# First block of a hybrid network in another order, and the first mixer tiles on what is unmasked

## The chip, the cores and the metric

One core of one Trainium2 chip computes all of it. The time is the device time in microseconds of that core for one execution. The kernel before was timed in three runs.

## The reference

`x` is 512 tokens by 1024 channels, in fp32. One first block is followed by two layers of a second kind. Cut to what matters here:

```python
def first_block(x, ...):
    z = rms_norm(x, norm1_g) @ w_in                    # 1024 -> 2304 columns
    y_a = gmlp_mixer(z[..., :512])                     # u * (masked ws @ layer_norm(gelu(v)))
    y_b = rglru_mixer(z[..., 512:768], z[..., 768:1024])  # convolution, gates, linear scan
    y_c = hgrn2_mixer(q, f, i, g)                      # att_ts = sum_d q_td k_sd exp(b_td - b_sd)
    y_d = pool_mixer(z[..., 2048:])                    # means over 2, 4, 8, 16 tokens
    x = x + concatenate([y_a, y_b, y_c, y_d]) @ w_out
    ...                                                # feed-forward, gated embedding

def hybrid_layer(x, ...):
    proj = rms(x) * norm1_g @ w_in
    o_a = sliding_window_attention(aq, ak, av, sinks) @ w_attn_o   # window 128, blocks of 128
    o_b = rwkv7_time_mix(rw, ...) @ w_rwkv_o
    o_c = retention(rq, rk, rv, rg) @ w_ret_o                      # chunks of 128, a running state
    x = x + (g0 * o_a + g1 * o_b + g2 * o_c) @ w_out
    ...                                                            # gated feed-forward
```

In the attention the first block of 128 queries sees no earlier block: its 128 keys before position 0 are masked. In the retention the state before the first chunk is zero, and the state after the last is not used.

## The kernel before, in words

Tensors lie with channels on 128 partitions and tokens in 512 columns. Every large weight comes as 128-column tiles of fp32. SP loads a tile pair into `raw` (two buffers, s = 0 and 1), POOL makes of it a rounded part `w_hi` (line 347) and a rest `w_lo` (line 354), and PE computes a *slot* (`slot`, three passes of eight matmuls, or of four where the input has four channel groups): `w_hi` by the input's high part, `w_hi` by its low part, `w_lo` by its high part, all summed in the accumulator `acc[s]`. Nearly all matmuls go through one helper, line 475. A slot may begin when POOL has split its weights (`w_split`) and DVE has emptied its accumulator (`acc_free`). A pair is the slots of s = 0 and 1.

The order of the work on each engine is written out by hand, and the engines meet at semaphores. In the first block, `w_in` has nine pairs, numbered 0 to 8. Their order is that of a list at the end of the file: input of the convolution, gate of the scan, `v` of the gated mixer, `u`, forget gate, query, value, output gate, input of the pooling. DVE empties the two accumulators of a pair one after the other in `take`. PE does pairs 1 and 2, the gates of the scan (`wa`, `wx`), pair 3, transposes of `v` (line 594), pairs 4 and 5, the mixing over time (`ws`), pairs 6 and 7, and then the seven levels of the forget-gated attention and an eighth round for the diagonal.

That attention is computed by levels: at level `lev`, tokens in the second half of a group of 2 x 2^lev see those in the first half. DVE makes differences of the running sum of log gates (`decays`), ACT turns them into factors (absolute value, exponential), DVE multiplies queries and keys with them (`decayed`), PE forms scores of all groups (round `lev`, semaphore `sc`), and DVE copies the chosen ones to `att` (`chosen`, copies with a predicate, line 1331; ACT copies those of levels 5 and 6). The differences of level lev + 1 are made in round lev. In between lie pair 8, four pairs of half of `w_out` on what is ready of the mixers' outputs (`yy`; DVE adds them to `x` in `partial`), and the states between chunks (`states`, `added`). Then come the end of that attention, the head sums (`headones`), and `late` and `slots` for the other half of `w_out`.

DVE's other steps there: the convolution (line 1200, three times two operations), 26 operations on two columns for the scan's constant (line 1206 to 1233, `lam` and `lp`), normalisation of `v` (to `vn`), and the scan itself (line 1279).

In a layer of the second kind, a retention over four chunks (`rt_`) and an attention over four tiles (`an_`) follow the third mixer, with projection slots for gates and outputs laid between their parts. `rt_R` is the running state, `rt_qx` the decayed queries, `rt_kz` the decayed keys, `an_s` the scores, `an_pT` the transposed probabilities.

```python
def slot(s, I, a, chunks, early=False):
    ...
    pe.wait_ge(w_split[s], I + 2)
    pe.wait_ge(acc_free[s], I + 1)
```

## Time and profile before

| | before |
| --- | --- |
| median of three runs | 2688.89 us (2687.46 to 2690.88) |
| profiled execution | 2691.99 us |
| span of the profile | 2690.2 us |
| mean granted clock of TensorE | 0.992 |
| DMA | 222.67 MB, 83 GB/s on average |

The profiled execution took 1.8 us more than its span and 3.1 us more than the median. In rows of a timeline stand the start and the duration in us, the engine, the line, the operation with output and inputs, how many instructions are merged in the row, and in brackets how long the engine stood idle before it and what ended that. One fp32 matmul appears as two records. The granted clock is a share of the full 2.4 GHz.

### The profile page before, as it was taken

To read this page: it belongs to the slowest core of one execution; us is meant where nothing else is said; L and a number is where in the kernel's file an instruction comes from. 1 tells how busy PE (TensorE), PEld (TensorE's weight loads), DVE (VectorE), ACT (ScalarE), POOL (GpSimd) and SP (SyncE) were. 2 spreads that over 40 slices of the span, in tenths; PEclk is the share of its full clock that TensorE was granted. 3 is DMA by queue.
4 is the path that set the end of the run, shared out by engine and by line. 5 is a ranking of instruction groups with operands and counts; after the bars stand their busy time and mean duration, and the time that the engine had idled before them with its cause. 6 is when DMAs were issued, how large, how long until landed. Compare 5 with 4: busy or idle time off the path is not lost.

```text
span 2690.2 us, 47577 instructions
## 1 busy us (share of the span) xinstructions
PE 2607.9 (97%) x16458; PEld 2037.5 (76%) x16458; DVE 1474.7 (55%) x2059; ACT 634.4 (24%) x1159; POOL 1488.9 (55%) x945
## 2 busy tenths in 40 slices
PE   7888999999999999999999999999999999999999
PEld 5776888877676677787888887776677777888887
DVE  6776737364566637774442424557647774443434
ACT  2333000013224423541200002234423431200002
POOL 4564565655544444546666665654444546666665
PEclk9999999999999999999999999999999999999999
DMA  4212333323321122223333333311122223333332
GB/s 151 67 44 86 94 94 94 94 86 92 93 64 49 40 90 63 66 73 93 94 94 94 94 94 108 94 57 48 49 84 67 71 73 96 94 94 94 94 94 94
DMA packets 72726, 222.67 MB, mean 83 GB/s; under 512 B 9345, under 2 KB 12545, under 8 KB 72577
## 3 DMA queue, kind: packets, MB, share of 16 engines
q1 hardware_dynamic: 72576, 220.63, 27.2%
q8 instruction: 100, 1.64, 0.3%
q14 instruction: 50, 0.40, 0.0%
HBM read 218.50 MB, written 2.10 MB: 82 GB/s over the span
## 4 chain that ended last, share of the span: by engine, by line
PE 89%; DVE 4%; DVEq 2%; issue 2%; DMA 1%; POOL 1%; POOLq 1%; ACT 1%; ACTq 0%; SPq 0%
PE acc L475 78%; PE bank L475 10%; DMA raw<-in_w_pg 1%; PE bank L1046 0%; POOL w_lo L354 0%; DVEq L1526 0%; DVE rw_bon L1084 0%; DVE rw_SCB L1084 0%; DVE z_rw L1084 0%; DVEq L1619 0%; DMA x<-in_x 0%; DVE rw_AR L1617 0%; POOL w_hi L347 0%; PE bank L1006 0%; DVE z_rw L1564 0%
## 5 line engine op out<-in xcount | busy, mean ns | idle before, releaser
L354 POOL TENSOR_TENSOR w_lo<-raw,w_hi 128x1024 fp32r<-128x1024 f32 (+3 forms) x438 | 966.0, 2206 | 302.7 <-PE acc L475 282.3
L347 POOL TENSOR_SCALAR w_hi<-raw 128x1024 fp32r<-128x1024 f32 (+3 forms) x438 | 431.9, 986 | 714.8 <-PE acc L475 604.7
L475 PE MATMUL acc<-xg_hi,w_hi 128*128 128x512 f32 x2224 | 597.2, 406 | 37.6 <-issue 16.7
L475 PE MATMUL acc<-xg_hi,w_lo 128*128 128x512 f32 x2224 | 587.9, 399 | 0.0
L475 PE MATMUL acc<-xg_lo,w_hi 128*128 128x512 f32 x2224 | 586.2, 399 | 0.0
L475 PEld LDWEIGHTS acc<-xg_hi,w_hi 128*128 128x128 f32 x2224 | 414.4, 190 | 156.2 <-issue 62.3
L475 PEld LDWEIGHTS acc<-xg_lo,w_hi 128*128 128x128 f32 x2224 | 417.6, 189 | 104.2 <-issue 5.1
L475 PEld LDWEIGHTS acc<-xg_hi,w_lo 128*128 128x128 f32 x2224 | 414.9, 188 | 99.9
L1899 ACT ACTIVATE ffn_act<-ffn_t 128x512 f32<-128x512 f32 x100 | 63.3, 633 | 778.2 <-DVEq L1144 619.6
L1084 DVE TENSOR_TENSOR x<-x,acc 128x512 f32<-128x512 f32 x104 | 71.4, 688 | 316.3 <-PE acc L475 315.6
L475 PE MATMUL acc<-hid_hi,w_hi 128*128 128x512 f32 x656 | 182.7, 396 | 3.7 <-POOL w_lo L354 1.6
L475 PE MATMUL acc<-hid_hi,w_lo 128*128 128x512 f32 x656 | 182.1, 395 | 0.0
L475 PE MATMUL acc<-hid_lo,w_hi 128*128 128x512 f32 x656 | 181.9, 395 | 0.0
L475 PEld LDWEIGHTS acc<-hid_hi,w_hi 128*128 128x128 f32 x656 | 123.1, 188 | 37.4 <-issue 6.8
L1084 DVE TENSOR_TENSOR ffn_sq<-acc,rstd 128x512 f32<-128x512 f32 x44 | 30.4, 692 | 212.3 <-PE acc L475 212.3
L475 PEld LDWEIGHTS acc<-hid_hi,w_lo 128*128 128x128 f32 x656 | 123.2, 188 | 29.9
L475 PEld LDWEIGHTS acc<-hid_lo,w_hi 128*128 128x128 f32 x656 | 123.2, 188 | 29.5
L1084 DVE TENSOR_TENSOR ffn_t<-acc,rstd 128x512 f32<-128x512 f32 x100 | 69.2, 692 | 125.1 <-PE acc L475 108.0
L1916 ACT ACT_TABLE_LOAD x96 | 123.2, 1283 | 5.0 <-issue 2.1
L1084 DVE TENSOR_TENSOR ffn_h<-ffn_act,ffn_sq 128x512 f32<-128x512 f32 x44 | 96.1, 2183 | 11.6 <-issue 11.6
L1899 ACT ACTIVATE ffn_act<-bank 128x512 f32<-128x512 f32 x22 | 13.2, 599 | 314.8 <-DVEq L1438 314.8
L457 POOL TENSOR_TENSOR x<-x,z_rt 128x1024 f32<-128x1024 f32 x8 | 19.0, 2377 | 119.9 <-DVEq L1526 119.9
(342 smaller groups left out, 2839.6 us busy)
## 6 DMA issues: line engine op xcount, KB each, us to landing
raw<-in_w_up SPq DMA_DIRECT2D x132, 512.0 KB, 3.6
raw<-in_w_down SPq DMA_DIRECT2D x48, 512.0 KB, 3.6
raw<-in_w_gate SPq DMA_DIRECT2D x48, 512.0 KB, 3.6
raw<-in_w_ret SPq DMA_DIRECT2D x32, 512.0 KB, 3.6
raw<-in_w_rw SPq DMA_DIRECT2D x28, 512.0 KB, 3.6
raw<-in_w_o SPq DMA_DIRECT2D x48, 256.0 KB, 2.6
raw<-in_w_in SPq DMA_DIRECT2D x18, 512.0 KB, 3.6
raw<-in_w_down SPq DMA_DIRECT2D x24, 384.0 KB, 3.0
```

Of the source, the lines that this page charges most:

```text
L347: nc.gpsimd.tensor_scalar(w_hi[:, s, 0:n], raw[:, s, 0:n], 1.0, 0.0, ALU.mult, ALU.add).then_inc(w_half[s], 1)
L354: nc.gpsimd.tensor_tensor(w_lo[:, s, 0:n], raw[:, s, 0:n], bits(w_hi[:, s, 0:n]), ALU.subtract).then_inc(w_split[s], 1)
L457: nc.gpsimd.tensor_tensor(x[:, 2 * j:2 * j + 2, :], x[:, 2 * j:2 * j + 2, :], z_rt[:, 15:16, :].to_broadcast([P, 2, T]), ALU.mult)
L475: return nc.tensor.matmul(o, a, b, start=first, stop=last, skip_group_check=shared)
L1084: return v.tensor_tensor(o, a, b, op)
L1899: return nc.scalar.activation(o, i, f, **kw)
L1916: nc.scalar.preload_act_table_set(name)
```

## The change

In the first block the forget gate's pair moves from fifth to third (number 2), the pairs of `v` and `u` follow it, and the log gates, their running sum and the differences of level 0 are made ahead of the normalisation of `v`. `take` empties one accumulator instead of two, and the two halves of a pair are taken at different places. Differences are made two levels ahead. Pairs 7 and 8 are done by PE one slot at a time in the first four level rounds, three pairs of `w_out` in rounds 4 to 6, and the fourth in two halves at the end. The transposes of the decayed keys and the states move to levels 4 and 5. The absolute value for the log gates is computed by ACT, where DVE computed it before, and ACT loads one more table; `gelu` and `silu` steps of ACT stand in another order. POOL splits the four pairs of `w_out` one place later each.

In the mixers of each layer: tile 0 of the attention leaves out its masked half (scores, maximum, exponentials, transposes, value products), chunk 0 of the retention leaves out the product with the zero state, and chunk 3 the update of the state. Two memsets go.

```diff
@@ -605,9 +609,10 @@
                     last = mm(bank[2 + 2 * k + j][:], K[name][:, j, :], m1["ta"][:, j, :], True, True)
             last.then_inc(s1["ri"], 1)
             pair(3)
-            pe.wait_ge(s1["z"], 3)
+            slot(0, 4, xg, full)
+            pe.wait_ge(s1["z"], 4)
             transposed(0, m1["tg"])
-            pair(4)
+            slot(1, 4, xg, full)
             pair(5)
...
             last.then_inc(s1["sv"], 1)
             pair(6)
-            pair(7)
...
-                    pair(8)
+                if lev < 4:
+                    slot(lev % 2, 7 + lev // 2, xg, full)
...
-                if 2 <= lev < 6:
-                    if lev == 2:
-                        pe.wait_ge(y_ready, 4)
-                    for s in range(2):
-                        slot(s, B1_IN + lev - 2, yy, four)
...
+                if 4 <= lev < 7:
+                    if lev == 4:
+                        pe.wait_ge(y_ready, 4)
+                    for s in range(2):
+                        slot(s, B1_IN + lev - 4, yy, four)
...
             last.then_inc(s1["dwy"], 1)
+            slot(0, B1_IN + 3, yy, four)
             for j in range(2):
                 pe.wait_ge(s1["osq"], j + 1)
                 head_sums(bank[j][:], m1["ta"][:, j, :]).then_inc(s1["on"], 1)
+            slot(1, B1_IN + 3, yy, four)
             rest = range(4, DC)
...
+                            seen = P if n == 0 else 0
+                            last = mm(bank[2 * p + j // 2][:, (j % 2) * 2 * P + seen:(j % 2 + 1) * 2 * P], z_at[r, j, n * P:(n + 1) * P],
+                                      an["k"][r, j // 2, n * P + seen:(n + 2) * P], True, True)
...
+                    if n < NT - 1:
+                        for j in range(4):
+                            last = nc.tensor.transpose(bank[4][:, j * P:(j + 1) * P], rt["kr"][:, j, :], K["ident"][:])
...
+                    if n > 0:
+                        for j in range(4):
+                            js = slice(j * P, (j + 1) * P)
+                            mm(bank[0][:, js], rt["R"][:, j, :], rt["qx"][:, j, :], j == 0, False, True)
...
+                    if n < NT - 1:
+                        for j in range(4):
+                            js = slice(j * P, (j + 1) * P)
+                            last = mm(bank[1][:, js], rt["kz"][:, js], rt["vt"][:, js], True, True)
...
-                            for b in range(2):
+                            for b in blocks(n):
                                 last = nc.tensor.transpose(bank[2 * p + j // 2][:, (2 * (j % 2) + b) * P:(2 * (j % 2) + b + 1) * P],
...
-                        for b in range(2):
+                        for b in blocks(n):
                             last = mm(bank[4][p * HD:(p + 1) * HD, j * P:(j + 1) * P], an["v"][:, b, kv * HD:(kv + 1) * HD],
-                                      an["pT"][:, 4 * p + j, b, :], b == 0, b == 1)
+                                      an["pT"][:, 4 * p + j, b, :], b == blocks(n)[0], b == 1)
...
-            def take(i, dst):
-
-                for s in range(2):
-                    scaled(s, i, dst[:, s, :]).then_inc(acc_free[s], 1)
-                dve.drain()
-                dve.sem_inc(s1["z"], 1)
-
-            take(0, z[:, 2:4, :])
+            def take(i, s, dst):
+
+                scaled(s, i, dst[:, s, :]).then_inc(acc_free[s], 1)
+                if s == 1:
+                    dve.drain()
+                    dve.sem_inc(s1["z"], 1)
...
@@ -1200,6 +1212,8 @@
                     v.scalar_tensor_tensor(m1["ta"][:, j, :], m1["td"][:, j, 13 + k:13 + k + T], col(U_CW + 4 * j + k),
                                            m1["ta"][:, j, :], ALU.mult, ALU.add)
                 dve.drain()
+                if k == 0:
+                    take(1, 0, z[:, 4:6, :])
             dve.sem_inc(s1["conv"], 1)
...
+            take(1, 1, z[:, 4:6, :])
...
-            take(2, m1["tg"])
+            zf = z[:, 8:10, :]
+            for s in range(2):
+                take(2, s, zf)
 
...
+            tt(m1["ta"][:], m1["ta"][:], z[:, 16:18, :])
             dve.drain()
             dve.sem_inc(s1["mlt"], 1)
-            take(3, z[:, 0:2, :])
...
+            take(3, 0, m1["tg"])
 
             dve.wait_ge(s1["sil"], 1)
-            v.scalar_tensor_tensor(m1["ta"][:], zf, 0.0, m1["tf"][:], ALU.min, ALU.subtract)
-            dve.drain()
+            v.scalar_tensor_tensor(m1["th"][:], zf, 0.0, m1["tf"][:], ALU.min, ALU.subtract)
+            take(3, 1, m1["tg"])
             lf = m1["td"][:, :, 0:T]
             for j in range(2):
-                v.tensor_tensor_scan(lf[:, j, :], K["reset128"][:], m1["ta"][:, j, :], 0.0, ALU.mult, ALU.add)
-
...
+                v.tensor_tensor_scan(lf[:, j, :], K["reset128"][:], m1["th"][:, j, :], 0.0, ALU.mult, ALU.add)
             dve.drain()
             dve.sem_inc(s1["free"], 1)
...
             decays(0)
-            take(6, m1["th"])
+            take(4, 0, z[:, 0:2, :])
+            dve.wait_ge(s1["scan"], 1)
+            tt(m1["tb"][:], m1["tb"][:], z[:, 16:18, :])
+            dve.drain()
+            dve.sem_inc(s1["hx"], 1)
...
+            take(4, 1, z[:, 0:2, :])
...
+            take(5, 0, z[:, 6:8, :])
+
...
             decays(1)
+            take(5, 1, z[:, 6:8, :])
+            tt(m1["tb"][:], m1["tb"][:], z[:, 4:6, :])
+            dve.drain()
+            for j in range(2):
+                splitted(y_hi[:, 2 + j, :], y_lo[:, 2 + j, :], m1["tb"][:, j, :])
...
+            tt(z[:, 0:2, :], m1["tg"][:], z[:, 0:2, :])
+            dve.drain()
+            take(6, 0, m1["th"])
+
+            dve.wait_ge(s1["qs"], 1)
             for lev in range(7):
-                dve.wait_ge(s1["hl"], lev + 2)
+                dve.wait_ge(s1["hl"], lev + 1)
                 if lev == 1:
                     dve.wait_ge(s1["vT"], 2)
                 decayed(lev)
-                dve.sem_inc(s1["qk"], 1)
-                if lev == 0:
-
-                    for j in range(2):
-                        splitted(y_hi[:, j, :], y_lo[:, j, :], m1["tg"][:, j, :])
-                    dve.drain()
-                    dve.sem_inc(y_ready, 4)
...
+                dve.sem_inc(s1["qk"], 2 if lev == 6 else 1)
                 if 0 < lev < 6:
                     chosen(lev - 1)
-                    decays(lev + 1)
-                if 2 < lev < 6:
-                    partial(lev - 3)
-                if lev == KV_LEV + 1:
-                    added(range(1))
-                if lev == KV_LEV + 2:
-                    added(range(1, NT - 1))
-            dve.sem_inc(s1["qk"], 1)
-            partial(3)
+                if lev == 0:
+                    take(6, 1, m1["th"])
+                if lev < 5:
+                    decays(lev + 2)
+                if lev in (1, 2):
+                    j = lev - 1
+                    splitted(y_hi[:, j, :], y_lo[:, j, :], z[:, j, :])
+                    dve.drain()
+                    dve.sem_inc(y_ready, 2)
+                    take(7, j, z[:, 10:12, :])
+                if lev in (3, 4):
+                    take(8, lev - 3, z[:, 12:14, :])
+                if lev == 5:
+                    partial(0)
+            added(range(NT - 1))
+            partial(1)
+            partial(2)
...
-                    tt(rt["qx"][:], rt["qr"][:], K["xi"][:])
+                    if n > 0:
+                        tt(rt["qx"][:], rt["qr"][:], K["xi"][:])
...
-                    mask = K["atmask"][:, n, :]
+                    seen = slice(0 if n else P, 2 * P)
+                    mask = K["atmask"][:, n, seen]
...
-    d["w1_in"] = slots(f["w_in"], [4, 5, 6, 7, 2, 3, 0, 1, 10, 11, 8, 9, 12, 13, 14, 15, 16, 17])
+    d["w1_in"] = slots(f["w_in"], [4, 5, 6, 7, 10, 11, 2, 3, 0, 1, 8, 9, 12, 13, 14, 15, 16, 17])
```

PE, ahead of the first round of scores. `ws,z` is the mixing over time, `m_tb,m_tc` the scores of level 0, `acc` rows are passes of slots. The kernel before, from the first pass of pair 7:

```order
L475 MATMUL acc<-xg_hi,w_hi 128x512 x8
L475 MATMUL acc<-xg_lo,w_hi 128x512 x8
L475 MATMUL acc<-xg_hi,w_lo 128x512 x8
L475 MATMUL acc<-xg_hi,w_hi 128x512 x8
L475 MATMUL acc<-xg_lo,w_hi 128x512 x8
L475 MATMUL acc<-xg_hi,w_lo 128x512 x8
L475 MATMUL bank<-m_tb,m_tc 128x128 x16
L594 MATMUL bank<-ident,m_th 128x128 x8
L475 MATMUL acc<-xg_hi,w_hi 128x512 x8
L475 MATMUL acc<-xg_lo,w_hi 128x512 x8
```

The changed kernel, from the last pass of pair 6:

```order
L479 MATMUL acc<-xg_hi,w_lo 128x512 x8
L479 MATMUL bank<-m_tb,m_tc 128x128 x16
L598 MATMUL bank<-ident,m_th 128x128 x8
L479 MATMUL acc<-xg_hi,w_hi 128x512 x8
L479 MATMUL acc<-xg_lo,w_hi 128x512 x8
L479 MATMUL acc<-xg_hi,w_lo 128x512 x8
L479 MATMUL bank<-m_tg,m_th 128x128 x16
L479 MATMUL acc<-xg_hi,w_hi 128x512 x8
L479 MATMUL acc<-xg_lo,w_hi 128x512 x8
```

Pair 7 no longer stands ahead of the scores, and one slot of it follows each of the first two rounds.

DVE, between the factors of the gates and the normalisation of `v` (`z,lng`). `acc,rstd` is one accumulator taken, `reset_65` the running sum of log gates. Before:

```order
L1238 TENSOR_SCALAR z<-z,sml 128x512 x2
L1084 TENSOR_TENSOR m_ta<-m_ta,m_te 128x1024
L1084 TENSOR_TENSOR z<-acc,rstd 128x512 x2
L1248 BN_STATS sml<-z 128x6 x4
L1251 BN_AGGR sml<-sml 128x2 x4
L1084 TENSOR_TENSOR z<-acc,rstd 128x512 x2
L1084 TENSOR_TENSOR m_tb<-m_tb,m_td 128x1024
L1261 TENSOR_SCALAR z<-z,sml 128x256 x4
L1084 TENSOR_TENSOR z<-z,lng 128x1024
L1084 TENSOR_TENSOR z<-z,lnb 128x1024
L1271 SCALAR_TENSOR_TENSOR m_tf<-z 128x1024
```

Now:

```order
L1095 TENSOR_TENSOR m_ta<-m_ta,z 128x1024
L1095 TENSOR_TENSOR m_tg<-acc,rstd 128x512
L1261 SCALAR_TENSOR_TENSOR m_th<-z,m_tf 128x1024
L1095 TENSOR_TENSOR m_tg<-acc,rstd 128x512
L1265 SCALAR_TENSOR_TENSOR m_td<-reset_65,m_th 128x512 x2
L1095 TENSOR_TENSOR m_tf<-m_td 128x512 x2
L1095 TENSOR_TENSOR z<-acc,rstd 128x512
L1095 TENSOR_TENSOR m_tb<-m_tb,z 128x1024
L1333 BN_STATS sml<-z 128x6 x4
L1336 BN_AGGR sml<-sml 128x2 x4
L1095 TENSOR_TENSOR z<-acc,rstd 128x512
L1342 TENSOR_SCALAR z<-z,sml 128x256 x4
```

The running sum and the first differences (`m_tf<-m_td`) now stand ahead of the normalisation; before they came twelve and fifteen rows behind `z,lng`.

## Rows read from the trace of the kernel before

**Rows 1.** The profile's page, part 1: busy time of the engines.
```profile
PE 2607.9 (97%) x16458; PEld 2037.5 (76%) x16458; DVE 1474.7 (55%) x2059; ACT 634.4 (24%) x1159; POOL 1488.9 (55%) x945
```

**Rows 2.** Windows: length, busy of PE, PEld, DVE, ACT, POOL; PEclk, DMA share, GB/s.
```profile
24.33:214.55 190.22, 162.49 (x895) 128.18 (x895) 141.35 (x187) 59.05 (x74) 102.79 (x69) 0.94 0.21 64
1000.00:1200.00 200.00, 199.05 (x1118) 155.88 (x1117) 152.49 (x213) 89.77 (x170) 93.22 (x67) 1.00 0.23 67
```

**Rows 3.** Timeline of PE, first block: start us, us, operation, idle before.
```profile
46.47 3.43 PE L475 MATMUL acc<-xg_hi,w_hi 128*128 128x512 f32 x8 [4.11 <-issue]
...
62.31 2.42 PE L475 MATMUL acc<-xg_hi,w_hi 128*128 128x512 f32 x8
...
107.74 3.75 PE L475 MATMUL acc<-xg_hi,w_hi 128*128 128x512 f32 x8 [8.52 <-issue]
...
115.20 2.03 PE L475 MATMUL acc<-xg_hi,w_hi 128*128 128x512 f32 x8
...
120.80 2.03 PE L475 MATMUL acc<-xg_hi,w_hi 128*128 128x512 f32 x8
...
152.86 3.56 PE L475 MATMUL bank<-m_tb,m_tc 64*128 64x128 f32 x32 [3.21 <-DVEq L1332]
...
162.67 2.06 PE L475 MATMUL bank<-m_tg,m_th 64*128 64x128 f32 x32
...
214.55 0.77 PE L475 MATMUL acc<-y_hi,w_hi 128*128 128x512 f32 x1 [2.96 <-DVE y_lo L1084]
```

**Rows 4.** Timeline of DVE, first block.
```profile
54.33 2.21 DVE L1233 TENSOR_SCALAR sml<-sml 128x2 f32<-128x2 f32 x1
...
86.99 2.87 DVE L1084 TENSOR_TENSOR m_tb<-m_tb,m_td 128x1024 f32<-128x1024 f32 x1
...
95.54 1.23 DVE L1084 TENSOR_TENSOR z<-z,lnb 128x1024 f32<-128x1024 f32 x1
96.89 1.86 DVE L1271 SCALAR_TENSOR_TENSOR m_tf<-z 128x1024 f32<-128x1024 f32 x1
...
109.48 1.22 DVE L1288 SCALAR_TENSOR_TENSOR m_ta<-z,m_tf 128x1024 f32<-128x1024 f32 x1
110.78 2.34 DVE L1292 TENSOR_TENSOR_SCAN m_td<-reset,m_ta 128x512 f32<-128x512 f32 x2
...
116.10 3.24 DVE L1084 TENSOR_TENSOR m_ta<-m_td 128x512 f32<-128x512 f32 x2 [0.17 <-issue]
...
126.02 2.06 DVE L1084 TENSOR_TENSOR m_tc<-m_ta,m_te 128x1024 f32<-128x1024 f32 x1
...
159.39 2.84 DVE L1331 COPY_PREDICATED att<-hgmask,bank 128x512 f32<-128x512 uint32 x4
...
177.37 1.53 DVE L1084 TENSOR_TENSOR m_tg<-m_tf,z 128x512 f32<-128x512 f32 x1 [0.88 <-ACT m_tf L1899]
...
190.55 0.90 DVE L1084 TENSOR_TENSOR m_tb<-m_ta,z 128x512 f32<-128x512 f32 x1
```

**Rows 5.** Timeline of POOL, first block.
```profile
54.09 2.43 POOL L354 TENSOR_TENSOR w_lo<-raw,w_hi 128x1024 fp32r<-128x1024 f32 x1 [0.82 <-PE acc L475]
```

**Rows 6.** Timeline of PE, mixers of the first layer.
```profile
1015.83 1.16 PE L475 MATMUL bank<-rt_qr,rt_kr 64*128 64x128 f32 x16 [0.53 <-DVEq L1765]
...
1020.22 1.05 PE L475 MATMUL bank<-rt_qx,rt_R 128*128 128x128 f32 x8
...
1090.55 0.66 PE L1006 MATMUL bank<-ident,rt_kr 128*128 128x128 f32 x4
...
1096.28 1.16 PE L475 MATMUL bank<-rt_vt,rt_kz 128*128 128x128 f32 x8
...
1103.83 2.00 PE L475 MATMUL bank<-an_k,z_at 64*128 64x256 f32 x16
...
1129.94 2.02 PE L475 MATMUL bank<-an_pT,an_v 128*64 128x128 f32 x32
...
1146.22 1.91 PE L1046 MATMUL bank<-ident,an_s 128*128 128x128 f32 x16
```

More of the change, by code:

```diff
@@ L274, in bits, with blocks @@
             return ap.bitcast(F32)
+        def blocks(n):
+            return (0, 1) if n else (1,)
         def tile_of(t, a, k, n):
@@ L1233, in _ @@
             v.tensor_scalar(lp[0], lp[0], 8.0, None, ALU.mult)
-            take(2, m1["tg"])
+            zf = z[:, 8:10, :]
+            for s in range(2):
+                take(2, s, zf)
             dve.wait_ge(s1["sig"], 1)
@@ L1807, in _ @@
                     say(s3, "osb")
-                    for p in range(2):
+                    for p in range(2 if n < NT - 1 else 0):
                         r = slice(p * HD, (p + 1) * HD)
@@ L1870, in _ @@
                         dve.drain()
-                        tt(an["s"][:, p], an["s"][:, p], bc(an["sum"][:, hs], 2 * P))
+                        tt(an["s"][:, p, :, seen], an["s"][:, p, :, seen], bc(an["sum"][:, hs], len(blocks(n)) * P))
                         say(s4, "pn")
@@ L1967, in _ @@
             for j in range(2):
[L1968 removed]
+                last = fn(z[:, 16 + j, :], bank[4 + j][:], ACT.Sigmoid, bias=vec[:, U_BX + j:U_BX + j + 1])
             last.then_inc(s1["sig"], 1)
[L1970 to L1976 removed]
+            act.wait_ge(s1["z"], 3)
+            fn(m1["te"][:], z[:, 8:10, :], ACT.Sigmoid, scale=-1.0)
+            table(LOG_EXP)
+            fn(m1["tf"][:], z[:, 8:10, :], ACT.Abs)
+            act.drain()
+            fn(m1["tf"][:], m1["tf"][:], ACT.Exp, scale=-1.0)
+            act.drain()
+            fn(m1["tf"][:], m1["tf"][:], ACT.Ln, bias=1.0).then_inc(s1["sil"], 1)
             table(EXP_TANH)
@@ L1986, in _, with decay @@
             fn(inv, inv, ACT.Exp, scale=-1.0).then_inc(s1["scan"], 1)
+            def decay(lev):
+                act.wait_ge(s1["ex"], lev + 1)
+                e = m1[("tf", "ta")[lev % 2]]
+                fn(e[:], e[:], ACT.Abs)
+                act.drain()
+                fn(e[:], e[:], ACT.Exp, scale=-1.0).then_inc(s1["hl"], 1)
+            decay(0)
+            table(GELU)
+            act.wait_ge(s1["vT"], 1)
+            for b in range(2):
+                last = fn(z[:, 14 + b, :], bank[b][:], ACT.Gelu_apprx_tanh)
+            last.then_inc(s1["act1"], 1)
+            table(LOG_EXP)
             act.wait_ge(s1["lv"], 1)
@@ new lines, in _ @@
+            decay(1)
+            decay(2)
+            act.wait_ge(s1["vT"], 2)
+            for b in range(2):
+                last = fn(z[:, 16 + b, :], bank[4 + b][:], ACT.Copy)
+            last.then_inc(s1["iev"], 1)
+            decay(3)
+            decay(4)
+            act.wait_ge(s1["ed"], 1)
+            fn(z[:, 8:10, :], z[:, 8:10, :], ACT.Exp)
+            fn(z[:, 14:16, :], m1["td"][:, :, 0:T], ACT.Exp)
+            for j in range(2):
+                last = fn(sml[:, 56 + 4 * j:60 + 4 * j], r3(m1["td"][:, j, 0:T], NT)[:, :, P - 1], ACT.Exp)
@@ L2028, in _ @@
+            last.then_inc(s1["edx"], 1)
+            decay(5)
+            decay(6)
+            act.wait_ge(s1["khT"], 1)
+            for n in range(NT - 1):
+                last = fn(states(n), bank[4 + n // 2][:, (n % 2) * 2 * P:(n % 2 + 1) * 2 * P], ACT.Copy)
+            last.then_inc(s1["khv"], 1)
+            table(SILU)
+            act.wait_ge(s1["z"], 8)
+            fn(z[:, 10:12, :], z[:, 10:12, :], ACT.Silu)
             for lev in (5, 6):
@@ L2037, in _ @@
                     last.then_inc(s1["sca"], 1)
-            table(SILU)
-            act.wait_ge(s1["z"], 8)
-            fn(z[:, 10:12, :], z[:, 10:12, :], ACT.Silu)
             table(LOG_EXP)
```

187 lines of the change are left out of this document (62 added, 125 removed).

## The prediction

> **What bounds the kernel now.** I read the page's busy times first, then the windows, then the timeline of PE in the first block, and last what DVE and POOL did where PE stood still. The reader is to see in the page that PE is busy for 97% of the span [rows 1], so at most 82 us of the 2690 are idle, and anything that does not take PE work or PE idle time away is worth nothing. In the windows two places count. In the first block, from 24.33 to 214.55 us, PE is busy for 162.5 of 190.2 us at a mean granted clock of 0.94 [rows 2]: 27.7 us of idle, and more lost to half rate. In the mixers of a layer, 1000 to 1200 us, PE is busy for 199 of 200 us at clock 1.00 [rows 2]: there the sum of PE's instructions is the time. In the timeline of PE the largest gaps of the first block are 4.11, 8.52, 3.21 and 2.96 us, ahead of 46.47, 107.74, 152.86 and 214.55 us [rows 3]; they are 18.8 of the 27.7, and the rest are a dozen short ones, most between the level rounds. After three of them the first pass is slow: 3.43 and 3.75 us for eight matmuls where a later one takes 2.03, 3.56 us for a round of scores where a later one takes 2.06 [rows 3]. That is the lower of the two granted levels (1.2 against 2.4 GHz) after standing still, 1.5 us each time; with the smaller spells I put the loss at six times 1.5 = 9 us. So 27.7 + 9 = 36.7 us of this stretch are not work at full rate, and the rest, 153.5 us, is work that the change keeps.
>
> **The first block, part by part.** I lay the new order out against these gaps.
>
> *Gap at 46 us.* PE has finished projection pair 1 and wants accumulator 0, which DVE only empties after the six steps of the convolution. The change takes accumulator 0 after the first two of them. The 4.11 us and the slow pass go: 5.6 us. What is late next is the taking of pair 2, which stays behind DVE's 26 small steps for `lam`. They ended at 54.33 + 2.21 = 56.54 us, the last of them, an operation on two columns, held for 2.21 us [rows 4] because POOL had begun a `w_lo` pass of 2.43 us at 54.09 [rows 5]. PE began pair 3 at 62.31 us [rows 3] and now stands ready for it 5.6 us earlier, at 56.7; the splits come earlier with it, so two `w_lo` passes instead of one can fall into the small steps. The chain then ends between 54.3 us (no pass meets it) and 59.0 (one more than before). With 0.7 us for the taking PE waits from 0 to 3 us, and loses 1.5 to the clock if it waits long. I take 3.0 + 1.5 = 4.5, since the pass that is shown held the chain for its whole length.
>
> The rule behind it is in the Trainium skill, SBUF — State Buffer, "Who interferes with whom": VectorE and GpSimd share one port pair, the one that issues first holds it for its whole instruction and the other fully blocks. With that rule the earlier splits cost the 4.5 us that I took, without it nothing and the forecast would be 2658. The trace agrees with it: 2.21 us for two columns.
>
> *Gap at 107 us.* PE waits for pair 5 to be taken, which DVE does behind the gated scan (accumulators in pairs: both wait). Now half of pair 5 is taken before the scan and half after it, when PE is still in pair 6. The 8.52 and 1.5 us go: 10.0 us. What is late next is the first round of scores. DVE's last step ahead of PE's `ws` matmuls ends at 96.8 us and its first level products at 126.02 + 2.06 = 128.1 us [rows 4], 31.3 us later. Of what lies between, the preparation of the forget gate (1.86 and 1.22 us), its scan (2.34) and the first differences (3.24) [rows 4] are now done earlier, where DVE waited for PE: 8.7 us, so 22.6 stay. The step ahead of `ws` comes near 92.8 us (PE is 1.1 us earlier there, 5.6 less 4.5, and the product `m_tb` by `m_td` of 2.87 us [rows 4] has been moved ahead of it), so level 0 is ready near 115.4. PE, at 5.6 us a slot (115.20 to 120.80 [rows 3]), began pair 6 at 107.74 - 8.52 = 99.2 without the gap; 1.1 earlier, and 11.2 long, it ends at 109.3. It waits 6.0 us and loses 1.5: 7.5. Bounds: 3, if DVE meets no POOL pass on the way, and 10, if it meets one at each of three more steps.
>
> *The level rounds.* Before, each round waited for ACT, since its differences were made only one level ahead: 0.88 us at 177.37 [rows 4], more at lower levels. A round took up to 13.2 us (177.37 to 190.55 [rows 4]), in which PE had one pair of 5.5 us and 2.06 us of scores. Now differences are two levels ahead, and a projection slot of 5.6 us lies after each of the first four rounds. PE has seven rounds of 7.6 us and some transposes, 58 us. DVE has two products (1.53 us for the first at 177.37), four predicated copies (2.84), a difference (3.24 at 116.10, part of it behind POOL) and one taking (0.7) [rows 4]: 7 to 9 us. So the two are level, and I leave PE 4 us of waits where the rounds cost 3.21 + 1.5 and most of the short gaps before. Bounds 1 and 10.
>
> *The end.* The last wait, 2.96 us at 214.55 [rows 3], is the chain scores, attention, head sums, ACT's root, DVE's halves. The two slots now put between its matmuls fill PE, but the chain itself gains a `partial` of two additions. I leave 4.4 us (bounds 3 and 7). Everything after 214.55 us is the same program.
>
> Left over: 4.5 + 7.5 + 4.0 + 4.4 = 20.4 us of the 36.7. The block gains **16 us**, with bounds of 8 (each term one half towards its bad end) and 25.
>
> ACT gets one more table load and an absolute value, about 2.4 us, in time in which it waits. SP's queue and POOL's number of splits are unchanged; three splits stand later among POOL's own steps.
>
> **The mixers, both layers.** On PE, per layer, by the rows: four `R` by `qx` matmuls in chunk 0 (1.05 us), four transposes of `kr` (0.66) and four `kz` by `vt` (1.16) in chunk 3, half of the scores of tile 0 (1.00 of 2.00), half of its value products (1.01 of 2.02) and half of its transposes (0.96 of 1.91) [rows 6]. That is 5.8 us; the last record of each group overlaps the next group by 0.1 to 0.25 us, so 4.9. DVE's `qx` product stood ahead of the rotated keys in chunk 0, for which PE waited 0.53 us [rows 6]; that may go as well, so bounds 4.4 and 5.8. I take 5.0 a layer, **10 us** for two. DVE loses two memsets and half of several operations; at 152 of 200 us [rows 2] it had room, so they count nothing.
>
> The eight transposes of attention and four of retention count here for 0.12 us each, from one group's busy time divided by its number [rows 6]. The Trainium skill, TensorE: Matmul & The Clock Gate, "PE-mode transpose", has some 275 ns for one in a kernel; by that figure, twelve fewer in two layers would be 6.6 us and the mixers would gain about 4 us more. The rows decide: sixteen records in 1.91 us.
>
> **Sum.** 16 + 10 = 26 us. The profiled execution took 2692.0 us, 3.1 above the median of the three timed runs; taken from it, 2666; from the median of 2688.9, **2663 us**.
>
> **Rivals.** *The order works better than laid out:* DVE's chain for `lam` is not held by POOL, level 0 is ready 3 us earlier and the end costs 3. Then 8 to 9 us more go: 2654.5. For it: ACT and DVE had idle stretches I did not count. Against it: the whole passes of POOL are in the rows.
> *The level rounds stay bound by DVE and POOL:* the differences keep costing over 3 us, as at 116.10, so that a round takes the 10.4 us it took before on average (six from 128.1 to 190.55 us [rows 4]). Seven of them are 73 us against 58 of PE work, 11 us more than I left; the block gains 5, the mixers 10: 2674. The Trainium skill, SBUF — State Buffer, "Who interferes with whom", says that the issue order and not the operation's shape decides who blocks; by that the same differences can cost either engine the wait, and it gives no time of its own.
> *Slower:* the same place, but every round longer than 13.3 us. At 14 us, seven rounds are 98 us, 36 more than I left; less 26 that is 10 us slower: 2699. It decides from 13.3 us a round on. The longest round of before was 13.2 us [rows 4] and held two states' additions, so all seven would have to be worse than the worst.
> *The mixers give nothing*, because DVE's masked softmax and not PE sets the time there: 2673. Against it stands a PE that is busy for 199 of 200 us.
>
> **How the numbers follow.** Forecast 0.68, better order 0.13, rounds bound by DVE 0.09, mixers nothing 0.04, slower 0.02, something in between or the projection's own gaps 0.04. A measurement of this kernel can tell about 0.2%, 5.4 us. All but the slower case and half of the last lie more than that below 2688.9. The range takes in the bounds of the block (8 and 25) with those of the mixers and most of the better order: 2653 to 2676.
>
> **What would show it.** In the profile after: the gap near 46 us gone, and one of 0 to 3 us before pair 3; no gap after the `ws` matmuls, and one of 3 to 10 us before the first scores, which start near 115 us instead of 132; rounds of 8 to 10 us without waits for ACT; the second pass over `y` starting near 198 us instead of 214.55. In the mixers the named groups gone or halved, and PE still over 99% busy. A first round of scores later than 120 us, or rounds of over 11 us, would prove the laying out wrong.

## The result and the profile after

The changed kernel takes 2667.7 us (median of four runs, 2665.7 to 2669.7) where the kernel before takes 2689.3 (four runs, 2687.5 to 2690.9). The ratio is 0.9918, with a 95% interval of 0.9902 to 0.9933: 22 us faster, between 18 and 26. The forecast was 2663, in a range of 2653 to 2676. The two profiled executions are 26.3 us apart (2692.0 and 2665.7), since that of before was longer than all its timed runs and that of after was the shortest of its own. 1.9 us of them lie ahead of all that was changed: the first sum of squares reaches PE at 22.41 us instead of 24.33, and in the profiles below it moves between 22.4 and 24.8 without an edit there. So I compare from that matmul on; the forecast's start times, laid out on the profile of before, are to be read 1.9 us earlier in the profile of after.

The page after, part 1, answers to [rows 1]:

```profile
PE 2592.7 (97%) x16370; PEld 2024.5 (76%) x16370; DVE 1457.7 (55%) x2041; ACT 632.8 (24%) x1159; POOL 1485.9 (56%) x945
```

PE has 15.2 us less to do (2607.9 to 2592.7) and stands still 11 us less (span less busy time: 82.3 to 71.2). The windows after answer to [rows 2] (length, busy time of PE, PEld, DVE, ACT and POOL, granted clock, DMA):

```profile
22.41:198.78 176.37, 156.89 (x896) 123.58 (x895) 143.97 (x185) 61.93 (x76) 99.90 (x69) 0.97 0.23 69
198.78:224.12 25.34, 23.07 (x91) 18.40 (x91) 15.94 (x26) 14.14 (x24) 15.24 (x15) 0.90 0.36 104
224.12:234.00 9.88, 9.88 (x34) 7.62 (x35) 1.29 (x2) 1.91 (x4) 5.50 (x4) 0.83 0.36 108
1000.00:1200.00 200.00, 199.79 (x1103) 156.68 (x1102) 145.00 (x208) 84.58 (x164) 99.37 (x72) 1.00 0.24 71
```

The first block is 176.4 us long instead of 190.2, 13.9 less, with PE's work at a mean clock of 0.97 instead of 0.94. Behind it, the unchanged stage of the second pass over `y` takes 25.34 us where it took 24.82, and from 224.12 us on the clock is at 0.83 of full rate where before it was at 1.00: the next sum of squares comes 7.18 us after that point instead of 5.68. These two give back 2.0 us. The block with what follows is worth 11.8.

The timeline of PE in the first block answers to [rows 3]:

```profile
57.58 2.10 PE L479 MATMUL acc<-xg_hi,w_hi 128*128 128x512 f32 x8 [2.52 <-issue]
...
92.80 1.97 PE L479 MATMUL bank<-ws,z 128*64 128x128 f32 x32 [0.52 <-DVEq L1347]
...
101.57 2.11 PE L479 MATMUL acc<-xg_hi,w_hi 128*128 128x512 f32 x8 [1.00 <-issue]
...
114.21 3.79 PE L479 MATMUL bank<-m_tb,m_tc 64*128 64x128 f32 x32 [6.79 <-DVEq L1286]
...
133.12 1.16 PE L479 MATMUL bank<-m_tb,m_tc 64*128 64x128 f32 x16 [0.61 <-DVEq L1294]
...
142.95 1.16 PE L479 MATMUL bank<-m_tg,m_th 64*128 64x128 f32 x16 [1.49 <-DVEq L1294]
...
152.39 1.16 PE L479 MATMUL bank<-m_tb,m_tc 64*128 64x128 f32 x16 [1.11 <-DVEq L1294]
...
161.18 2.06 PE L479 MATMUL bank<-m_tg,m_th 64*128 64x128 f32 x32
...
198.78 0.76 PE L479 MATMUL acc<-y_hi,w_hi 128*128 128x512 f32 x1 [4.21 <-DVE y_lo L1095]
```

The gaps of 4.11 and 8.52 us are gone. Four are left: 2.52 us ahead of pair 3, 6.79 ahead of the first scores, with the lower clock behind it (3.79 us for a round that takes 2.06), short ones for the copies at L1294, and 4.21 us for the last halves of `y`. What DVE did ahead of two of them, and behind one (its timeline):

```profile
46.41 2.52 DVE L1095 TENSOR_TENSOR sml<-sml 128x2 f32<-128x2 f32 x2
...
52.04 2.20 DVE L1241 TENSOR_SCALAR sml<-sml 128x2 f32<-128x2 f32 x1
...
56.80 1.28 DVE L1095 TENSOR_TENSOR z<-acc,rstd 128x512 f32<-128x512 f32 x2
...
73.99 4.08 DVE L1095 TENSOR_TENSOR m_tf<-m_td 128x512 f32<-128x512 f32 x2
...
108.69 2.40 DVE L1095 TENSOR_TENSOR z<-m_tg,z 128x1024 f32<-128x1024 f32 x1
...
119.24 1.23 DVE L1095 TENSOR_TENSOR m_tg<-m_ta,z 128x1024 f32<-128x1024 f32 x1 [2.88 <-PE bank L598]
```

and POOL's, which holds the small steps:

```profile
46.28 2.39 POOL L358 TENSOR_TENSOR w_lo<-raw,w_hi 128x1024 fp32r<-128x1024 f32 x1 [0.82 <-PE acc L479]
...
51.88 2.34 POOL L358 TENSOR_TENSOR w_lo<-raw,w_hi 128x1024 fp32r<-128x1024 f32 x1 [0.88 <-PE acc L479]
```

Two passes of `w_lo` now fall into the chain for `lam`, as the forecast said one or two would. The mixers of layer 1 on PE, answering to [rows 6]:

```profile
1001.58 1.16 PE L479 MATMUL bank<-rt_qr,rt_kr 64*128 64x128 f32 x16
...
1006.06 1.09 PE L479 MATMUL bank<-rt_ST,rt_vt 128*64 128x128 f32 x16
...
1087.07 1.16 PE L479 MATMUL bank<-an_k,z_at 64*128 64x128 f32 x16
...
1105.33 1.04 PE L1057 MATMUL bank<-ident,an_s 128*128 128x128 f32 x8
1106.12 1.17 PE L479 MATMUL acc<-y_hi,w_hi 128*128 128x512 f32 x4
...
1111.02 1.09 PE L479 MATMUL bank<-an_pT,an_v 128*64 128x128 f32 x16
```

The `R` by `qx` group of chunk 0 is gone, scores, transposes and products of tile 0 are halved, and the wait of 0.53 us is gone. Counted between the same matmuls, the traces part by 6.2 us in the first layer and 6.1 in the second.

### The profile page after: what moved, and what is told of

The parts are those of the page before. It is cut to its first block, busy times and chain, and to the rows that moved or that the text cites. A ratio compares the mean times of both kernels' runs of the same rounds, so it can differ in the third digit from the quotient of the medians.

```text
span 2663.9 us, 47379 instructions
## 1 busy us (share of the span) xinstructions
PE 2592.7 (97%) x16370; PEld 2024.5 (76%) x16370; DVE 1457.7 (55%) x2041; ACT 632.8 (24%) x1159; POOL 1485.9 (56%) x945
## 4 chain that ended last, share of the span: by engine, by line
PE 89%; DVE 5%; DVEq 3%; issue 1%; DMA 1%; POOL 1%; ACT 0%; SPq 0%; ACTq 0%; POOLq 0%
PE acc L479 78%; PE bank L479 10%; DMA raw<-in_w_pg 1%; POOL w_lo L358 0%; PE bank L1057 0%; DVE z L1095 0%; DVEq L1538 0%; DVE rw_bon L1095 0%; DVEq L1275 0%; DVEq L1631 0%; DVE rw_SCB L1095 0%; DVE z_rw L1095 0%; DVE att L1293 0%; DVEq L1294 0%; DVEq L1286 0%
```

## The experiments

All ran beside the kernel before, whose medians there were 2690.4 to 2691.5 us. Each ratio is to it; the changed kernel's is 0.9918. The intervals are about 0.0015 to either side, 4 us, so a difference of less than 5 to 6 us between two of my kernels is not shown by time alone. "Block" is the time in the profile from the first sum of squares to the second: 220.7 us before, 208.9 after. It carries 1.5 us of chance at each of two places, where the same wait is followed by the lower clock in some profiles and by the full one in others (last section).

**Each part alone.** e1 puts the mixers' edits on the kernel before, e2 takes them out of the changed kernel.

```diff
-                    for j in range(4):
-                        js = slice(j * P, (j + 1) * P)
-                        mm(bank[0][:, js], rt["R"][:, j, :], rt["qx"][:, j, :], j == 0, False, True)
+                    if n > 0:
+                        for j in range(4):
+                            js = slice(j * P, (j + 1) * P)
+                            mm(bank[0][:, js], rt["R"][:, j, :], rt["qx"][:, j, :], j == 0, False, True)
...
```

> The kernel before with the edits of the mixers alone (first tiles on what is unmasked); the first block as before. Theory: the two traces differ by 6.2 us in layer 0 and 6.1 in layer 1, and since PE is busy for over 99% there, all of it is time: 12.3 us faster than before, near 2677. Rival: the forecast's 10 us is right and the rest of the difference is noise of one profile each: 2679. A second rival: some of the 12.3 comes only because the first block ends earlier; then under 8 us, over 2681.

> The changed kernel with the mixers as before: the new order of the first block alone. Theory: by the two traces the block gives 15.8 us at the second pass over y, of which 1.9 are from an earlier start of the first matmuls that the change does not touch, and 1.5 are given back to the slow clock at the next two stages: 12 us, near 2677, and e1 and this one add up to the change's 21.6 to 26. Rival: the block gives the 16 us of the forecast: 2673. Rival two: part of the mixers' 12.3 depends on the order, so the two parts don't add up, by over 3 us.

Measured: e1 2677.8 us, ratio 0.9953 (0.9939 to 0.9966), 12.7 us; e2 2679.4, ratio 0.9956 (0.9942 to 0.9969), 11.8 us. They add up to 24.5 against the change's 22, within the intervals, so neither is seen to need the other. The mixers are worth what the traces say; by time they are worth 9 to 16 us, which takes in the forecast's 10, so that it is more is said by the traces alone. The block gives 12, between 8 and 15.6, and so a little less than 16.

**Undoing: differences one ahead.**

```diff
-                if lev < 5:
-                    decays(lev + 2)
+                if 0 < lev < 6:
+                    decays(lev + 1)
```

> The changed kernel with the level differences made one level ahead again instead of two. Theory by the forecast: each round then waits for the differences (2.6 to 3.7 us on DVE), ACT's two activations (2.1) and the products (1.4), over the copies, so that rounds 2 to 5 take about 3 us more each: 8 to 12 us slower than the changed kernel, 2676 to 2680. Rival: DVE, which is busy for 9 of 9.7 us in rounds 1 to 3, sets the length either way, and ACT's answer comes beside the copies: under 3 us, below 2671.

Measured: 2673.7 us, ratio 0.9931 (0.9918 to 0.9945), block 215.7: 3.5 us slower than the changed kernel by the ratios, 6.0 by the medians, 6.8 in the block, 1.4 of which are a slower pass ahead of pair 3 that the edit does not touch (3.48 us against 2.10). About half of what I expected, and at the edge of what the times can tell. DVE waits for ACT only 0.15 us in two early rounds, 1.47 in the next two and 0.87 in one more. The largest new wait is PE's, at another place:

```profile
160.09 1.63 PE L479 MATMUL acc<-y_hi,w_hi 128*128 128x512 f32 x4 [3.54 <-issue]
```

Its cause is two queues away, in POOL's timeline of the same run:

```profile
152.38 2.38 POOL L386 TENSOR_TENSOR z<-z,m_te 128x1024 f32<-128x1024 f32 x1 [12.88 <-ACT sml L1910]
...
158.71 1.27 POOL L358 TENSOR_TENSOR w_lo<-raw,w_hi 128x512 fp32r<-128x512 f32 x1 [0.17 <-issue]
```

ACT's exponentials for the chunks' ends stand behind its level 4, which now comes a round later; POOL waits for them, and the first split for `y` stands behind POOL's wait. PE starts at 160.09, when that split (158.71 + 1.27 = 159.98) is done.

**Undoing: pairs 1 and 5 in pairs.**

```diff
-                if k == 0:
-                    take(1, 0, z[:, 4:6, :])
...
-            take(1, 1, z[:, 4:6, :])
+            for s in range(2):
+                take(1, s, z[:, 4:6, :])
...
-            take(5, 0, z[:, 6:8, :])
...
-            take(5, 1, z[:, 6:8, :])
+            for s in range(2):
+                take(5, s, z[:, 6:8, :])
```

> The changed kernel with accumulators of pairs 1 and 5 taken in pairs again (behind the convolution, behind the gated scan). By the forecast's terms, each gap is back at 4.1 and 8.5 us with the slow clock (15.6 us), but the waits left over in the changed kernel (2.5 us before pair 3, 6.8 and 1.7 before the first scores) are swallowed by them: 4 to 6 us slower, 2672 to 2674. Rival: PE comes later everywhere and DVE's chain too, since it needs PE's ws matmuls and transposes: the whole 15 us, 2683. Rival two: DVE alone sets the first scores, so that both gaps are hidden there: under 2 us, 2668 to 2670.

Measured: 2667.9 us, ratio 0.9914 (0.99 to 0.9927), block 209.1: no difference that the times can tell. PE's timeline shows both gaps back, 4.12 and 5.95 us with their slow passes, and no wait before the first scores:

```profile
46.82 3.51 PE L479 MATMUL acc<-xg_hi,w_hi 128*128 128x512 f32 x8 [4.12 <-issue]
...
105.98 3.75 PE L479 MATMUL acc<-xg_hi,w_hi 128*128 128x512 f32 x8 [5.95 <-issue]
...
119.79 2.06 PE L479 MATMUL bank<-m_tb,m_tc 64*128 64x128 f32 x32
```

From its first sum of squares (24.67) the first scores start 95.1 us later, against 91.8 after the change, and run at full rate. 2.5 us of this delay reach the second pass over `y` (203.51, 178.8 us after the sum of squares, against 176.4), and 1.7 the first matmul of the stage behind it (228.10, 203.4 us after it, against 201.7). At the next sum of squares only 0.2 are left, but that is chance: the last stretch ahead of it took 5.68 us here, at full rate, and 7.18 in the changed kernel. So taking the accumulators of pairs 1 and 5 singly moves most of PE's idle time from two places to one, and is worth some 2 us by the profile; the time can tell neither this nor the 3.6 us of the forecast from nothing.

**More for PE to do before the first scores.** e4a puts a slot ahead of them and the three after it one round earlier, and DVE's takings with them. e4b moves the slots over `y` too.

```diff
             pair(6)
+            slot(0, 7, xg, full)
...
-                if lev < 4:
-                    slot(lev % 2, 7 + lev // 2, xg, full)
+                if lev < 3:
+                    slot((lev + 1) % 2, 7 + (lev + 1) // 2, xg, full)
...
-                if 4 <= lev < 7:
+                if 3 <= lev < 6:
...
```

The last edit is e4b's alone.

> The changed kernel with the first accumulator slot of pair 7 (5.6 us of PE work) put ahead of the first scores, in the 6.8 us in which PE stands still, and the three slots after it one round earlier each; DVE takes the accumulators earlier to match. Theory one, DVE sets the length of rounds 1 to 4 (9.8, 9.8, 9.5 and 7.3 us with PE busy for 8.1 of 9.5): the 5.6 us only move, PE stands still in round 3 instead, and what is won is the slow clock of the first scores and what follows it, 1.5 to 2.5 us: 2665 to 2666. Theory two, PE's work sets the time of this stretch: 5.6 us and the slow clock, 6 to 7 us: 2661. The profile: the wait before the first scores below 2 us in both.

> The same, and the slots over y moved one round earlier too (rounds 3 to 5 instead of 4 to 6), so that the room in round 3 is filled and the last round holds none. Theory one (DVE sets rounds 1 to 4, PE and the wait for its slots the end: DVE stood 3.9 and 2.1 us for the accumulators of pair 2 of y ahead of the chosen copies of level 7): the 5.5 us come out at the end, 6 to 8 us in all: 2660 to 2662. Theory two: the end hangs on ACT's copies, the chosen copies and the attention chain, which do not start earlier: 2 us or less. Theory three: the rounds get longer by the added work of POOL falling on DVE: nothing or slower.

e4a: 2668.4 us, ratio 0.9917 (0.9904 to 0.9931), nothing, and its block is longer (212.1). The 5.6 us only moved. Its waits on PE are now 3.86 us before the first scores and 6.51 in round 3, which has no slot:

```profile
119.86 3.25 PE L479 MATMUL bank<-m_tb,m_tc 64*128 64x128 f32 x32 [3.86 <-DVEq L1287]
...
158.47 3.46 PE L479 MATMUL bank<-m_tb,m_tc 64*128 64x128 f32 x32 [6.51 <-DVEq L1295]
```

So theory one holds for the rounds, though the 1.5 to 2.5 us that I hoped for did not show; the wait before the scores, for which I had said under 2 us, stayed at 3.86, since DVE is as late as before. e4b: 2680.4 us, ratio 0.9963 (0.9949 to 0.9977), 12 us slower than e4a. My third theory allowed for "nothing or slower", but from POOL's work falling on DVE, which is not what the profiles below show.

**Two readings of e4b's waits.** PE stood 3.0, 3.3 and 5.7 us ahead of the slots over `y`, all put down to "issue". I took them for POOL's splits and moved these one place up (e5), and then moved DVE's additions of pairs 0 and 1 one round up as well (e9).

> The kernel of e4b_slots_one_earlier (2680.4 us) with POOL's splits for y one place earlier each among POOL's own steps, as in the kernel before. In e4b PE waited 3.0, 3.3 and 5.7 us ahead of the three slots over y, with DVE and the scores ready; I read it as waits for those splits, which stood behind POOL's wait of 11.5 us for ACT's decays to the chunk's end. Theory one, the splits' place is the cause: the three waits go (12 us, and the slow clock after each, 1.5 apiece) and the time comes to 2662 to 2668. Theory two, one buffer of split weights per accumulator is the cause (a split cannot begin before the slot before it is done): then a good part of the waits stays and the time is 2670 to 2680.

> The kernel of e5_pool_order (2683.6 us) with DVE's additions of the first two pairs over y one round earlier too (rounds 4 and 5 instead of 5 and behind the states). In e5 and e4b PE still stood 6.1 and 5.7 us ahead of the second and third slot over y although POOL's splits were done; each time the slot began about a microsecond after DVE's additions into x, which I had left in their places. Theory one, these additions are what PE waited for: both waits go, and with them the slow clock behind each, 15 us in all: 2666 to 2669, and if the last round without a slot brings the end forward, down to 2662. Theory two, POOL's splits or their single buffer hold PE: no change, 2680 or more.

```diff
-                if lev == 5:
-                    partial(0)
+                if lev in (4, 5):
+                    partial(lev - 4)
             added(range(NT - 1))
-            partial(1)
             partial(2)
```

e5: 2683.6 us, ratio 0.9969 (0.9957 to 0.9981). My reading was wrong for two of the three: the first wait went, the others stayed at 6.10 and 5.69. e9: 2665.6 us, ratio 0.9905 (0.9888 to 0.9921), and both are gone. DVE's and PE's rows of e4b show what they were:

```profile
166.26 1.28 DVE L1096 TENSOR_TENSOR x<-x,acc 128x512 f32<-128x512 f32 x2
...
182.81 1.29 DVE L1096 TENSOR_TENSOR x<-x,acc 128x512 f32<-128x512 f32 x2
```

```profile
167.06 1.58 PE L479 MATMUL acc<-y_hi,w_hi 128*128 128x512 f32 x4 [3.32 <-issue]
...
183.60 2.05 PE L479 MATMUL acc<-y_hi,w_hi 128*128 128x512 f32 x4 [5.68 <-issue]
```

Each slot starts 0.8 us after DVE begins the two additions that free the accumulators. I had moved PE's slots and not the steps of DVE that empty what they fill. With them moved (e9 keeps e5's splits too) the 12 us lost in e4b are back. Against the changed kernel e9 is 2 us faster by the medians and 3.5 by the ratios, which is within the noise, and its block is no shorter (209.6).

**DVE's chain before the first scores.** e10 splits chunks 2 and 3 of `y`, and forms the product for chunks 0 and 1, in round 0 and not ahead of level 0.

```diff
-            tt(m1["tb"][:], m1["tb"][:], z[:, 4:6, :])
+            tt(z[:, 4:6, :], m1["tb"][:], z[:, 4:6, :])
             dve.drain()
-            for j in range(2):
-                splitted(y_hi[:, 2 + j, :], y_lo[:, 2 + j, :], m1["tb"][:, j, :])
...
-            tt(z[:, 0:2, :], m1["tg"][:], z[:, 0:2, :])
-            dve.drain()
...
+                if lev == 0:
+                    tt(z[:, 0:2, :], m1["tg"][:], z[:, 0:2, :])
+                    dve.drain()
+                    for j in range(2):
+                        splitted(y_hi[:, 2 + j, :], y_lo[:, 2 + j, :], z[:, 4 + j, :])
```

> The changed kernel with two pieces of DVE's work moved out of the way of the first scores: the product into z (2.4 us) and the four steps that split chunks 2 and 3 of y (3.0 us) now come in round 0, where DVE stood 2.9 us for PE's transposes. Theory one, DVE's chain sets the first scores and all behind them: PE's wait before them falls from 6.8 to 1 to 2 us, the whole chain of rounds starts 5.4 us sooner and keeps 3 to 5 of them: 2663 to 2665. Theory two, DVE's work is only moved, and rounds 0 and 1 get longer by what was moved: under 1 us, 2667 to 2668.

Measured: 2663.2 us, ratio 0.9896 (0.9879 to 0.9912). The wait fell to 3.80 us:

```profile
113.26 3.67 PE L479 MATMUL bank<-m_tb,m_tc 64*128 64x128 f32 x32 [3.80 <-DVEq L1286]
```

The scores start 88.8 us after the sum of squares instead of 91.8: 3.0 sooner and not 5.4, because the second level product now takes 3.36 us where it took 1.22. DVE's row and the pass of POOL that began just before it:

```profile
109.82 3.36 DVE L1095 TENSOR_TENSOR m_tc<-m_tf,m_te 128x1024 f32<-128x1024 f32 x1
```

```profile
109.71 2.38 POOL L358 TENSOR_TENSOR w_lo<-raw,w_hi 128x1024 fp32r<-128x1024 f32 x1 [0.88 <-PE acc L479]
```

It is 4.5 us faster than the changed kernel by the medians and 6 by the ratios, at the edge of what can be told, and the block is only 0.6 us shorter (208.3) in its one profile, which was its slowest run (2668.0). The numbers lean to theory one: what leaves DVE's chain ahead of the scores is time, what is given to PE there (e4a, e8) is little or nothing. The profile of e11 below bears it out better.

**The end of the block.** e6 cuts ACT's root and DVE's last steps chunk by chunk.

```diff
-            partial(3)
-            dve.wait_ge(s1["o"], 1)
-            tt(m1["tb"][:], m1["tb"][:], m1["ta"][:])
...
+            partial(3, (0,))
+            for j in range(2):
+                dve.wait_ge(s1["o"], j + 1)
+                tt(m1["tb"][:, j, :], m1["tb"][:, j, :], m1["ta"][:, j, :])
...
+            partial(3, (1,))
...
-            act.drain()
-            fn(m1["ta"][:], m1["ta"][:], ACT.Exp, scale=-0.5).then_inc(s1["o"], 1)
+                act.drain()
+                fn(m1["ta"][:, j, :], m1["ta"][:, j, :], ACT.Exp, scale=-0.5).then_inc(s1["o"], 1)
```

> The changed kernel with the end of the first block cut finer: ACT's root and DVE's four steps of the last two chunks of y go chunk by chunk, and the second addition of partial(3), for which DVE stood 0.74 us and which took 0.69, comes after them. Theory one: PE's wait of 4.21 us and the slow clock after it (eight single matmuls at 0.63 instead of 0.39, 1.5 to 2 us) hang on this chain; the first half of y is ready 3 us earlier and PE waits under 2 us: 3 to 5 us faster than the changed kernel, 2663 to 2665. Theory two: the clock is low there anyway, since PE stands still a little in any case: 2 us. Rival: the later addition holds slot 1 instead: nothing.

Measured: 2666.0 us, ratio 0.9913 (0.9899 to 0.9927): 1 to 2 us, less than the 3 to 5 of theory one, and not told from nothing by time. The wait is cut into two:

```profile
199.00 0.47 PE L479 MATMUL acc<-y_hi,w_hi 128*128 128x512 f32 x1 [1.89 <-DVE y_lo L1095]
...
201.70 0.47 PE L479 MATMUL acc<-y_hi,w_hi 128*128 128x512 f32 x1 [1.75 <-DVE y_lo L1095]
```

They add up to 3.6 us against 4.21, and the slow passes come behind them instead; the block is 209.3.

**Together.** e11 is e10 with e6, e12 is e11 with the slots, splits and additions of e9.

> The edits of e10_scores_sooner and of e6_end_chain together, on the changed kernel. If the two are apart in place they add up: e6 gave 1 to 2 us, so 1 to 2 us less than e10, 2661 to 2664 in theory one. If e10 gives nothing, this gives what e6 gave, 2666.

> The edits of e9_takes_to_match, e10_scores_sooner and e6_end_chain together, the last candidate. With the slot of pair 7 ahead of the first scores PE has 5.6 us more to do there, where e10 leaves it 3.8 us to wait. Theory one, the parts are apart: e11 stands at 2663.5, e9 gave 2 to 3.5 us over the changed kernel, so 2660 to 2662. Theory two, e9 and e10 fill the same hole (the wait before the first scores), so that the one takes what the other would give: 2663 to 2665, no better than e11.

e11: 2663.5 us, ratio 0.9899 (0.9883 to 0.9916), the same time as e10: e6's 1 to 2 us do not show. Its block is 204.7, 4.2 us shorter than the changed kernel's, and these two profiles agree in the clock at both of the places where chance comes in. The scores start 3.0 us sooner here too (88.8 us after the sum of squares); e6's part is about 1 us (its block less the slower pass ahead of pair 3), so the 3 us are kept to the end of the block. e12: 2661.0 us (2660.3 to 2661.5), ratio 0.989 (0.9874 to 0.9907), 29 us faster than before; all its four runs lie below the changed kernel's shortest. It is 2.5 us below e11 by the medians, which the times do not tell from nothing, and its block (205.8) is no shorter. In its profile no wait is left before the first scores, which run at full rate.

```profile
115.46 2.06 PE L479 MATMUL bank<-m_tb,m_tc 64*128 64x128 f32 x32
...
127.15 3.69 PE L479 MATMUL bank<-m_tg,m_th 64*128 64x128 f32 x32 [3.02 <-DVEq L1295]
```

The next round waits 3.02 us instead: the rounds stay DVE's.

## Why the prediction was right, and where it was off

The sign, the size and the places held: 26 us forecast, 22 measured. By the traces the block gave 4 us less than its 16 and the mixers 2 us more than their 10. These two misses partly cancel, which is luck. By its steps:

- *Gap at 46 us.* Gone, and 2.52 us are left ahead of pair 3, for the cause given, two passes of POOL in the chain for `lam`; I had 3.0 for the wait and 1.5 for the clock, and the pass behind it ran at full rate (2.10 us). Right in kind, 2 us too much in this profile; 1.5 of them are chance, since in six of the eleven profiles with this order the pass took 3.0 us or more.
- *Gap at 107 us.* Gone. I had 6.0 us of wait before the first scores and a start near 115 us; it is 6.79, with 1.7 for the clock, and 114.21, which is 116.1 counted as in the profile of before.
- *Of both.* My terms gave these two removals 15.6 us and took back 12.0, net 3.6. e8 puts the net at some 2 us by its profile, and by time at nothing that can be told: the gaps were for the most part idle time of an engine that had to wait for DVE's chain further on. That the net was small is what the forecast had right.
- *The level rounds.* 4 us of waits forecast; 3.85 in the six short ones at L1294, and 0.59 before the attention matmuls. Rounds of 8 to 10 us forecast; they are 10.5, 8.5, 9.8, 9.4, 8.8, 9.0 and 7.7 from one start of scores to the next.
- *The end.* 4.4 us left in all, forecast; the wait is 4.21, and the six single matmuls and the pass behind them run at the lower clock, which costs some 2 us more (5.50 us from 198.78 to the third pass of four, against 3.2 at full rate). This term was 2 us too small. The second pass over `y` starts at 198.78 us, and forecast was near 198; but counted as in the profile of before it is 200.7, 2.2 us late, 0.7 of which are already there at the first scores. That the two figures look alike is the earlier start of this profile.
- *"Everything after 214.55 us is the same program."* This step failed in size. It is the same program, and it took 2.0 us longer: at 224.12 us the clock fell to 0.83 for the 10 us that ran at 1.00 before. That part (1.5 us) is not shown to be a price of the new order: in e4a, e8 and e9, which have it too, this stretch took 5.68 us as before.
- The block's 16 us are 13.9 to the point where I summed, and 11.8 behind it; e2 measures 11.8, between 8 and 15.6.
- *The mixers.* 5.0 us a layer forecast, 6.2 measured (e1: 12.7 us for both). I had subtracted overlaps of 0.9 us from records of 5.8. Between starts the groups give 5.2: 1.0 (`R` by `qx`), 0.4 and 0.9 (chunk 3), 0.8 (scores), 1.1 (transposes), 1.0 (products). The rest are three waits of 0.53, 0.23 and 0.18 us, of which I named one and priced it only in the bound.
- *The price of a transpose.* Eight took 0.79 us from their start to that of the next group (1105.33 to 1106.12), 0.10 each, near the row's 0.12. By the figure of the Trainium skill, TensorE: Matmul & The Clock Gate, "PE-mode transpose", some 275 ns for one (measured there in bf16), my estimate for the mixers would have been 14 us and not 10. The measured 12.7, with its interval of 9 to 16, excludes neither; the rows decide for the small price.
- *POOL before DVE.* The forecast drew on the Trainium skill, SBUF — State Buffer, "Who interferes with whom", that whichever issues first holds the port; the page says this of VectorE in a two-port mode, and of a step of VectorE with two inputs in SBUF only that it contends with GpSimd's reads. The trace agrees for two such steps: two TENSOR_TENSOR on two columns took 2.52 us beside a `w_lo` pass that began at 46.28. A TENSOR_SCALAR took 2.20 beside that of 51.88; in which mode it ran, no row shows.
- *Rivals.* "Rounds bound by DVE and POOL" was priced at 2674 and came out at half its mechanism: DVE does set the rounds (e4a), but at 9 and not 10.4 us a round. The mixers giving nothing, and the slower case, are excluded by e1 and by the rounds' lengths.

Of the block's 12 us, two-ahead differences are 4 to 6 (e7), with the noise of the times beside it. The rest belongs to the new order (forget gate third, its scan and first differences in DVE's idle time, slots in the rounds). I did not take this apart: the order of the projections is tied to every wait behind it.

## What to carry to other kernels

The widest gap of the busiest engine is not its price: ask which engine's chain ends the next wait, since filling such a gap with nothing else changed mostly moves the idle time to that wait (e8, e4a), while the 3 us taken out of that chain were kept to the end of the block (e10's edits, in the profile of e11). When a producer's steps are moved, move with them what empties their buffers, on every engine; "issue" in a wait may be an accumulator not yet freed. A gap that a forecast leaves is to be priced with the clock behind it, and one profile is not enough to read 1.5 us of that from.

## What was unexpected

The clock after one and the same short wait is not the same from run to run. Ahead of pair 3 PE stood still 2.52 to 2.54 us in the eleven profiles that have the same order up to there. The eight matmuls behind took 2.10 us in five of them, the changed kernel's and e10's among them, and 3.00 to 3.66 in the other six (3.00 in e9, 3.37 in e12), as in e4a:

```profile
59.03 3.66 PE L479 MATMUL acc<-xg_hi,w_hi 128*128 128x512 f32 x8 [2.53 <-issue]
```

So a stall of this length costs 0 to 1.6 us more, with no difference ahead of it that I can see. The second place is the stretch ahead of the next sum of squares, where PE waits some 2 us in every profile. It took 5.7 us in five of the fourteen profiles (before, e1, e4a, e8, e9) and 7.2 in the other nine. Its first matmul in the changed kernel and in e8:

```profile
224.12 0.76 PE L479 MATMUL acc<-xg_hi,w_hi 128*128 128x512 f32 x1 [2.27 <-DVE xg_lo L1095]
```

```profile
228.10 0.48 PE L479 MATMUL acc<-xg_hi,w_hi 128*128 128x512 f32 x1 [2.15 <-DVE xg_lo L1095]
```

With a dozen such places this may be a part of the 4 to 9 us by which the runs of most of these kernels differ; I did not test that.
